# Eight token-major projections of a two-part transformer kernel, taken two weight units at a time with 512 moving columns

## The chip, the cores and the metric

The kernel runs as one program on one core of a Trainium2 chip. The metric is the device time of one execution in microseconds (us), and lower is better. The page and the trace describe one profiled execution; the time before is a median over three executions that were not profiled.

## What is computed

The input is one sequence of 256 tokens with 1024 features and a memory of the same size. A first block of two layers (modulated feed-forward, a mixer of three kinds, feed-forward) is followed by a second block of four layers. Only the second block is touched by the change. Each of its layers is a mixer, a cross attention and a feed-forward, all in fp32:

```python
def second_block(x, mem, ...):
    mem_n = rmsnorm(mem, norm_mem)
    for i in range(DEPTH_2):                        # 4 layers
        hn = rmsnorm(x, norm_mix[i])
        if kind == 0:   mix = diff_attention(hn, da_w_in[j], da_w_out[j], ...)   # q, k, v = split(h @ w_in)
        elif kind == 1: mix = hgrn2(hn, hg_w_in[j], hg_w_out[j], ...)            # q, f, i, g = split(h @ w_in)
        else:           mix = chunked_sgu(hn, sg_w_in[j], sg_w_out[j], ...)      # u, v = split(gelu(h @ w_in))
        x = x + mix
        x = x + mem_cross_attention(rmsnorm(x, norm_cross[i]), mem_n, ca_w_q[i], ca_w_kv[i], ca_w_o[i])
        x = x + swiglu(rmsnorm(x, norm_ffn[i]), ffn_w_gu[i], ffn_w_down[i])
```

Layers 0 and 3 have the differential attention, layer 1 the gated recurrence (hgrn2), layer 2 the gating unit (sgu).

## The kernel before, in words

**Weights in units.** All weight matrices pass through a ring of four slots (`raw`, `whi`, `wlo`; `SLOTS = 4`). A unit is 256 columns of a matrix with 1024 rows: 128 partitions times 2048 elements, 1 MB. For each unit SP (the sync engine) starts a DMA into `raw`. ACT (ScalarE) rounds it to fp32r into `whi` (line 667) and DVE (VectorE) writes the rest, raw minus the rounded value, into `wlo` (line 971). Activations are kept in the same two parts (`hhi`, `hlo`; for the memory `mhi`, `mlo`). A product is then three fp32r matmuls: high by high, high by low, low by high.

**When a unit is split.** ACT and DVE each walk through the same list of stages in program order. At each unit `u` they call `ahead(u.pos)`, which splits units up to three positions ahead. The unit at position `p + 3` lies in the slot that unit `p - 1` used. Both engines therefore wait for `used` of unit `p - 1`, the semaphore that PE (TensorE) raises with that unit's last matmul. DVE waits for ACT's `whi` too. After this call the engine waits for `used` of unit `p` and copies its PSUM bank out (`take_out`). On each engine these things happen strictly one after the other.

**Projections.** `project` runs the units of one projection on PE; `unit` does one of them. Most are feature-major: the weights are stationary and the 256 tokens move (lines 1511 to 1513). Eight are token-major: a 128-token slice of the activations is stationary and the 256 weight columns move (lines 1542 to 1544). They are `dv` in layers 0 and 3, `hv` in layer 1, `sv` in layer 2 and `xv`, the values of the cross attention, in all four layers. Each has four units, and each unit has 48 matmuls: two token tiles, eight row tiles, three products. The two token tiles fill the two halves of one PSUM bank, the bank of the unit's slot. DVE copies `dv`, `hv` and `xv` out (line 1181), ACT copies `sv` out through Gelu (line 767). The first block has token-major units too (`c_v`, `mv`), with the same function.

**What follows a token-major projection.** After `dv` PE starts the attention (`diff`, scores at lines 1791 and 1792), after `hv` the recurrence (`tree8`, line 1684). Both first wait for `all_read`, that is, for every bank of the stage to be copied out. After `sv`, stage `sgu`, ACT waits for the same, squares `sv` (line 906) and takes a root of the sum (lines 909 and 911). DVE meanwhile masks a weight (line 1437), PE turns it (line 1502), DVE copies it (line 1440) and then scales `sv` (line 1444). After `xv` the units of `xq` follow, and nothing waits for the copies at once.

Of the kernel before, what the change touches and what calls it, by code (L numbers as in the profile page):

```python
# [25 lines left out]
ACT = mybir.ActivationFunctionType  # L26
AX = mybir.AxisListType

P = 128
D = 1024  # L30
KT = D // P
S = 256
ST = S // P
# [176 lines left out]
def build(nc, a, out):  # L210

    ctx = ExitStack()
    with ctx:
        def sb(name, shape, dt=F32):
            return ctx.enter_context(nc.sbuf_tensor(name, shape, dt))

        def sem(name):
            return ctx.enter_context(nc.semaphore(name))
# [3 lines left out]
        whi = sb("whi", [P, SLOTS, UNIT], F32R)  # L222
        wlo = sb("wlo", [P, SLOTS, UNIT], F32R)
# [21 lines left out]
        ps = ctx.enter_context(nc.psum_tensor("ps", [P, 8, 512], F32))  # L245
# [13 lines left out]
        def work(at, *dims):  # L259
            n = int(np.prod(dims))  # L260
            v = W[:, at:at + n]
            if len(dims) == 2:
                return v.rearrange("p (a b) -> p a b", a=dims[0])
            if len(dims) == 3:
                return v.rearrange("p (a b c) -> p a b c", a=dims[0], b=dims[1])
            return v
# [30 lines left out]
        dq, dk, dv = work(0, KT, S), work(2048, KT, S), work(4096, ST, D)  # L297
# [3 lines left out]
        hq, hk, hf, hv = work(0, KT, S), work(2048, KT, S), work(4096, KT, S), work(6144, ST, D)  # L301
# [3 lines left out]
        su, sv = work(0, KT, S), work(2048, ST, D)  # L305
# [3 lines left out]
        xk, xv, xq = work(2048, KT, S), work(4096, ST, D), work(6144, KT, S)  # L309
# [6 lines left out]
        used = [sem(f"unit_used{i}") for i in range(SLOTS)]  # L316
        read = [sem(f"bank_read{i}") for i in range(SLOTS)]
        q = {n: sem(n) for n in (
            "const_in mem_in token_in rows_in misc_in bias_out aux_in "
            "rows_turned misc_turned bias_mm vec_copied tok_turned tok_copied pro_v pro_s c_ready "  # L320
            "ada_sum ada_red ada_col "
            "norm_sq norm_ss norm_ln norm_rs norm_gain norm_t norm_hi norm_lo "
            "ffn_hi ffn_lo ffn_scale x_new "
            "gn_sq gn_ss gn_ln gn_rs gn_out rope_mm rope_cos rope_done "
            "gate_mm gate_s gate_v taps_v conv_mm conv_v conv_s conv_hi conv_lo "
            "scores_mm masked maxed exped scaled probs turned_mm turned values_mm values_hi values_lo "
# [62 lines left out]
        for l in range(DEPTH1):  # L389
# [3 lines left out]
            w = a["mix_w_in"][l]  # L393
# [13 lines left out]
        for i in range(DEPTH2):  # L407
            norm("norm_mix_2", i, ready, 2)
            j = i // 3
            if i % 3 == 0:  # L410
                w = a["da_w_in_2"][j]
# [6 lines left out]
            elif i % 3 == 1:  # L418
                w = a["hg_w_in_2"][j]
# [9 lines left out]
            else:  # L429
                w = a["sg_w_in_2"][j]  # L430
# [33 lines left out]
        def bank_read(u):  # L464
            return read[u.slot], u.read + 1

        def product_of(u):
            return used[u.slot], u.use + 1

        def split_ahead(split):  # L470


            at = [0]
            last = {}

            def ahead(pos, far=AHEAD):
                while at[0] < n_stream and at[0] <= pos + far:
                    s, use, _, size = plan.stream[at[0]]
                    if last.get(s, -1) >= max(pos, 0):
                        return  # L480
                    split(s, use, size)
                    last[s] = at[0]
                    at[0] += 1
            return ahead
# [32 lines left out]
        def rows2(v):  # L517
            return v.rearrange("p (a b) -> p a b", a=2)
# [125 lines left out]
        @block_.gpsimd  # L644
        def _(pool):
            nc.gpsimd.memset(gate_w[96:128, :, :], 0.0).then_inc(q["pro_s"], 1)
            for s, use, _, size in plan.stream:
                if s in LO_ON_DVE:
                    continue

                pool.wait_ge(hi_done[s], use + 1)
                if use > 0:
                    pool.wait_ge(used[s], use)
                nc.gpsimd.tensor_tensor(wlo[:, s, 0:size], raw[:, s, 0:size], whi[:, s, 0:size].bitcast(F32),
                                        ALU.subtract).then_inc(lo_done[s], 1)
# [3 lines left out]
        def _(act):  # L659
# [63 lines left out]
            def ffn(st):  # L723
# [23 lines left out]
                "hq": (ACT.Silu, 1.0, lambda i: hq[:, 2 * i:2 * i + 2, :]),  # L747
                "hgate": (ACT.Silu, 1.0, lambda i: h_gate[:, 2 * i:2 * i + 2, :]),
                "su": (ACT.Gelu, 1.0, lambda i: su[:, 2 * i:2 * i + 2, :]),
                "sv": (ACT.Gelu, 1.0, lambda i: sv[:, :, 256 * i:256 * i + 256]),  # L750
                "xk": (ACT.Copy, 1.0, lambda i: xk[:, 2 * i:2 * i + 2, :]),
                "xq": (ACT.Copy, 0.0625, lambda i: xq[:, 2 * i:2 * i + 2, :]),
            }
# [206 lines left out]
        def _(dve):  # L960
            v = nc.vector
# [186 lines left out]
            def outp(st):  # L1148
# [13 lines left out]

            COPIES = {
                "c_v": lambda i: c_v, "mv": lambda i: mv[:, :, 256 * i:256 * i + 256],
                "dv": lambda i: dv[:, :, 256 * i:256 * i + 256], "hv": lambda i: hv[:, :, 256 * i:256 * i + 256],
                "xv": lambda i: xv[:, :, 256 * i:256 * i + 256],
            }

            def take_out(u):
                ahead(u.pos)  # L1170
                name, i = u.what
                if name == "hf":

                    dve.wait_ge(*bank_read(u))
                    for k in (2 * i, 2 * i + 1):
                        ts(hf[:, k, :], hf[:, k, :], lower[:, 1, k:k + 1], lower[:, 0, k:k + 1], ALU.mult, ALU.add)
                        m = ts(hk[:, k, :], hk[:, k, :], lower[:, 1, k:k + 1], None, ALU.mult)
                    m.then_inc(q["mix_f"], 1)
                if name in COPIES:
                    dve.wait_ge(*product_of(u))  # L1180
                    v.tensor_copy(COPIES[name](i), rows2(ps[:, u.slot, :])).then_inc(read[u.slot], 1)
# [315 lines left out]
        def _(pe):  # L1497
            mm = nc.tensor.matmul
# [5 lines left out]
            def weights(u):  # L1504
                pe.wait_ge(hi_done[u.slot], u.use + 1)
                pe.wait_ge(lo_done[u.slot], u.use + 1)

            def product(dst, w, xh, xl, first, last):

                wh, wl = w  # L1510
                mm(dst, wh, xh, start=first, stop=False)  # L1511
                mm(dst, wh, xl, start=False, stop=False)  # L1512
                return mm(dst, wl, xh, start=False, stop=last)  # L1513

            def tiles(slot, cols=256):

                return [t[:, slot, 0:KT * cols].rearrange("p (k m) -> p k m", k=KT) for t in (whi, wlo)]

            def h_parts(src):
                return (mhi, mlo) if src == "mem" else (hhi, hlo)  # L1520

            def unit(u, src, h, extra=()):
                weights(u)

                if u.read > 0:
                    pe.wait_ge(read[u.slot], u.read)
                for e in extra:
                    pe.wait_ge(*e)
                if src == "mem":
                    pe.wait_ge(q["norm_lo"], 8)  # L1530
                xh, xl = h_parts(src)
                th, tl = tiles(u.slot, u.cols)
                for m in range(u.cols // P if not u.token_major else ST):
                    for k in range(KT):
                        if src == "h" and h is not None and m == 0:

                            pe.wait_ge(q["norm_lo"], 8 * h + k + 1)
                        c = slice(P * m, P * m + P)
                        dst = ps[:, u.slot, 256 * m:256 * m + 256]
                        if u.token_major:  # L1540
                            first, last = k == 0, k == KT - 1
                            mm(dst, xh[:, k, c], th[:, k, :], start=first, stop=False)  # L1542
                            mm(dst, xh[:, k, c], tl[:, k, :], start=False, stop=False)  # L1543
                            o = mm(dst, xl[:, k, c], th[:, k, :], start=False, stop=last)  # L1544
                        else:
                            o = product(dst, (th[:, k, c], tl[:, k, c]), xh[:, k, :], xl[:, k, :], k == 0, k == KT - 1)
                o.then_inc(used[u.slot], 1)

            def ada_pair(u, s=0):

                pe.wait_ge(q["ada_sum"], 8 * (u + 2))
                for c in range(2):
                    for t in range(2):
                        at = 2 * (u + c) + t
                        dst = ps[:, 3, at:at + 1] if isinstance(u, int) else ps[:, 3, bass.ds(at, 1)]
                        o = mm(dst, ada_acc[:, 2 * s + c, P * t:P * t + P], ones[:, 0:1], start=True, stop=True)
                o.then_inc(q["ada_red"], 2)
# [104 lines left out]
                outs(STEPS - 1, last=True)  # L1662

            def project(st):
                for n, u in enumerate(st.units):
                    unit(u, st.src, st.h, st.free if n == 0 else ())

            def group_sum(g, bank, src, what):
                pe.wait_ge(q["gn_sq"], g + 1)
# [243 lines left out]
```

## Time and profile before

| | |
|---|---|
| time, median of 3 runs | 3364.84 us (3359.9 to 3366.36) |
| the profiled execution, own time | 3366.07 us |
| its span, first to last instruction | 3364.3 us |
| outside the span | 1.8 us |
| mean granted TensorE clock | 0.928 of full speed |
| busy PE / DVE / ACT | 87% / 55% / 42% of the span |

In the rows below, PE is TensorE's matmul, PEld its weight load, which runs beside it. A matmul's duration in the trace is longer than its share of the stream, since matmuls overlap; what a matmul costs is the distance from its start to the start of the next one. PEclk is the granted clock as a share of full speed: 1.00 is 2.4 GHz and 0.50 is 1.2 GHz. "L1181" is a line of the kernel.

### The profile page before, as it was taken

Reading aid. Unit: us, or ns where it says so; the run is one execution under the profiler, and the core shown is the slowest. Engines: PE = TensorE matmul, PEld = TensorE weight load, DVE = VectorE, ACT = ScalarE, POOL = GpSimd, SP = SyncE. Lnnn points to the kernel's source line nnn. Section 1 sums busy time; section 2 is a strip of 40 time slices with the busy share of each in tenths; the row PEclk is TensorE's granted clock in tenths of the full one; section 3 lists DMA queues with packets and bytes.
Section 4 is the critical chain, followed back from the end, with each engine's and each line's share of the span. In section 5 each row is a group of like instructions: output and inputs, shape, how many; then the busy total and the mean of one; then the engine's idle time right before and its main releaser. Section 6 shows DMA issues by size and latency. Waiting matters only on the chain.

```text
span 3364.3 us, 53426 instructions
## 1 busy us (share of the span) xinstructions
PE 2940.6 (87%) x22527; PEld 2827.3 (84%) x22527; DVE 1841.3 (55%) x2554; ACT 1403.1 (42%) x1620; POOL 0.7 (0%) x5
## 2 busy tenths in 40 slices
PE   3898878989987799859899877999889898969898
PEld 2898858989985799849899876899889898859898
DVE  5786756868758444544444563444444445444443
ACT  3334534344354433454433414444434444344433
POOL 0000000000000000000000000000000000000000
PEclk6899979999997899969999998999989999979999
DMA  6896306968851265515264513345534356414353
GB/s 182 272 299 217 113 26 230 301 206 286 270 181 33 85 204 175 176 37 162 71 206 162 177 54 110 101 150 187 175 126 138 115 185 198 140 50 138 118 183 100
DMA packets 458657, 533.07 MB, mean 158 GB/s; under 512 B 9863, under 2 KB 434937, under 8 KB 458489
## 3 DMA queue, kind: packets, MB, share of 16 engines
q1 hardware_dynamic: 458489, 530.76, 48.7%
q8 instruction: 114, 1.87, 0.2%
q14 instruction: 54, 0.44, 0.0%
HBM read 528.10 MB, written 2.62 MB: 158 GB/s over the span
## 4 chain that ended last, share of the span: by engine, by line
PE 80%; DVE 10%; ACT 5%; DMA 3%; issue 2%; SPq 1%; DVEq 0%; ACTq 0%
PE ps L1511 17%; PE ps L1512 17%; PE ps L1513 17%; PE ps L1640 15%; PE ps L1602 2%; PE ps L1544 2%; PE ps L1543 2%; PE ps L1542 2%; PE ps L1684 2%; DVE work L1093 1%; DVE wlo L971 1%; DMA bias_rows<-raw 1%; DVE work L1258 1%; DMA work<-in_ada_w 1%; PE ps L1670 1%
## 5 line engine op out<-in xcount | busy, mean ns | idle before, releaser
L1511 PE MATMUL ps<-hhi,whi 128*128 128x256 f32 x4528 | 1309.9, 289 | 134.9 <-DVE hlo L1103 85.6
L971 DVE TENSOR_TENSOR wlo<-raw,whi 128x2048 fp32r<-128x2048 f32 (+1 forms) x514 | 976.3, 1920 | 763.0 <-ACT whi L667 762.8
L1512 PE MATMUL ps<-hlo,whi 128*128 128x256 f32 x4528 | 1301.3, 287 | 0.0
L1513 PE MATMUL ps<-hhi,wlo 128*128 128x256 f32 x4528 | 1300.4, 287 | 0.0
L667 ACT ACTIVATE whi<-raw 128x2048 fp32r<-128x2048 f32 (+1 forms) x514 | 824.9, 1613 | 683.5 <-PE ps L1513 396.8
L1511 PEld LDWEIGHTS ps<-hhi,whi 128*128 128x128 f32 x4528 | 891.1, 197 | 150.7 <-issue 150.0
L1512 PEld LDWEIGHTS ps<-hlo,whi 128*128 128x128 f32 x4528 | 890.9, 197 | 1.0 <-issue 1.0
L1513 PEld LDWEIGHTS ps<-hhi,wlo 128*128 128x128 f32 x4528 | 889.9, 197 | 0.0
L1640 PE MATMUL ps<-ghi,whi 128*128 128x256 f32 x1408 | 400.1, 284 | 12.3 <-DVE glo L1119 9.7
L1640 PE MATMUL ps<-glo,whi 128*128 128x256 f32 x1408 | 399.1, 283 | 0.0
L1640 PE MATMUL ps<-ghi,wlo 128*128 128x256 f32 x1408 | 399.0, 283 | 0.0
L1640 PEld LDWEIGHTS ps<-ghi,whi 128*128 128x128 f32 x1408 | 270.9, 192 | 13.7 <-DVE glo L1119 11.0
L1640 PEld LDWEIGHTS ps<-glo,whi 128*128 128x128 f32 x1408 | 271.0, 192 | 0.0
L1640 PEld LDWEIGHTS ps<-ghi,wlo 128*128 128x128 f32 x1408 | 271.0, 192 | 0.0
L730 ACT ACTIVATE work<-ps 128x512 f32<-128x512 f32 x88 | 52.6, 598 | 383.3 <-PE ps L1513 383.3
L1056 DVE SCALAR_TENSOR_TENSOR work<-work,silu_c 128x256 f32<-128x256 f32 x504 | 202.6, 478 | 0.0
L767 ACT ACTIVATE work<-ps 128x512 f32<-128x512 f32 (+1 forms) x74 | 43.8, 592 | 323.4 <-PE ps L1513 310.0
L1602 PE MATMUL ps<-work,con 128*128 128x256 f32 x320 | 101.8, 488 | 57.8 <-ACT work L703 57.8
L1602 PEld LDWEIGHTS ps<-work,con 128*128 128x128 f32 x320 | 79.0, 253 | 77.3 <-ACT work L703 40.5
L738 ACT ACTIVATE ghi<-work 128x512 fp32r<-128x512 f32 x88 | 55.8, 634 | 178.0 <-PE ps L1640 145.2
L1116 DVE TENSOR_TENSOR work<-work,ps 128x512 f32<-128x512 f32 x88 | 60.4, 686 | 123.8 <-PE ps L1513 110.2
L1119 DVE TENSOR_TENSOR glo<-work,ghi 128x512 fp32r<-128x512 f32 x88 | 60.8, 691 | 80.9 <-ACT ghi L738 80.9
(225 smaller groups left out, 2921.3 us busy)
## 6 DMA issues: line engine op xcount, KB each, us to landing
raw<-in_ffn_w_in SPq DMA_DIRECT2D x88, 1024.0 KB, 8.8
raw<-in_ffn_w_gu SPq DMA_DIRECT2D x88, 1024.0 KB, 5.0
work<-in_ada_w SPq DMA_DIRECT2D x72, 1024.0 KB, 8.7
raw<-in_ffn_w_out SPq DMA_DIRECT2D x88, 512.0 KB, 5.6
raw<-in_ffn_w_down SPq DMA_DIRECT2D x88, 512.0 KB, 5.4
raw<-in_ca_w_kv SPq DMA_DIRECT2D x32, 1024.0 KB, 5.4
raw<-in_mix_w_in SPq DMA_DIRECT2D x24, 1024.0 KB, 5.5
raw<-in_da_w_in SPq DMA_DIRECT2D x24, 1024.0 KB, 5.2
```

The source lines that it names most:

```text
L667: f(whi[:, s, 0:size], raw[:, s, 0:size], ACT.Copy).then_inc(hi_done[s], 1)
L971: tt(wlo[:, s, 0:size], raw[:, s, 0:size], whi[:, s, 0:size].bitcast(F32), ALU.subtract).then_inc(lo_done[s], 1)
L1056: m = stt(acc, w, silu_c[:, k:k + 1], acc, ALU.mult, ALU.add)
L1511: mm(dst, wh, xh, start=first, stop=False)
L1512: mm(dst, wh, xl, start=False, stop=False)
L1513: return mm(dst, wl, xh, start=False, stop=last)
L1542: mm(dst, xh[:, k, c], th[:, k, :], start=first, stop=False)
L1543: mm(dst, xh[:, k, c], tl[:, k, :], start=False, stop=False)
L1544: o = mm(dst, xl[:, k, c], th[:, k, :], start=False, stop=last)
L1602: o = mm(ps[:, st.bank, 0:S], ones, norm_x[:, k, :], start=k == 0, stop=k == KT - 1)
L1640: o = mm(dst, a_, b_[:, t, :], start=first and t == 0 and i == 0 and m % 2 == 0, stop=last and t == 1 and i == 2 and m % 2 == 1, skip_grou ...
L1684: o = mm(d[:, c], K[rows_, tile, c], Q[rows_, tile, c], start=True, stop=True)
```

## The change

Within the eight token-major projections of the second block, two neighbouring units are now done together. A new function `unit_pair` waits for the weights and the banks of both units. It then takes the token tiles as the outer loop, and each matmul moves 512 columns: 256 of one slot and 256 of the next. Token tile 0 goes to the bank of the first slot, tile 1 to the bank of the second. Only the very last product of a pair is done as two matmuls of 256 columns, and these raise `used` for the two units. `take_out` copies one bank per token tile, with as many elements as before. The units of the first block keep the old function.

```diff
-                "sv": (ACT.Gelu, 1.0, lambda i: sv[:, :, 256 * i:256 * i + 256]),
+                "sv": (ACT.Gelu, 1.0, lambda i: sv[:, i % 2, 512 * (i // 2):512 * (i // 2) + 512]),
...
-                "dv": lambda i: dv[:, :, 256 * i:256 * i + 256], "hv": lambda i: hv[:, :, 256 * i:256 * i + 256],
-                "xv": lambda i: xv[:, :, 256 * i:256 * i + 256],
             }
+            PAIRED = {"dv": dv, "hv": hv, "xv": xv}
...
+                if name in PAIRED:
+                    t, c = i % 2, 512 * (i // 2)
+                    dve.wait_ge(*product_of(u))
+                    v.tensor_copy(PAIRED[name][:, t, c:c + 512], ps[:, u.slot, :]).then_inc(read[u.slot], 1)
...
+            def unit_pair(u, v, src, h, extra=()):
+                weights(u)
+                weights(v)
+                for w in (u, v):
+                    if w.read > 0:
+                        pe.wait_ge(read[w.slot], w.read)
...
+                xh, xl = h_parts(src)
+                s = u.slot
+                th, tl = (w[:, s:s + 2, :].rearrange("p s (k m) -> p s k m", k=KT) for w in (whi, wlo))
+                for t in range(ST):
+                    c = slice(P * t, P * t + P)
+                    for k in range(KT):
+                        if src == "h" and h is not None and t == 0:
+                            pe.wait_ge(q["norm_lo"], 8 * h + k + 1)
+                        mm(ps[:, s + t, :], xh[:, k, c], th[:, :, k, :], start=k == 0, stop=False)
+                        mm(ps[:, s + t, :], xh[:, k, c], tl[:, :, k, :], start=False, stop=False)
+                        if t == 0 or k < KT - 1:
+                            mm(ps[:, s + t, :], xl[:, k, c], th[:, :, k, :], start=False, stop=k == KT - 1)
+                            continue
+                        for n, w in enumerate((u, v)):
+                            mm(ps[:, s + t, 256 * n:256 * n + 256], xl[:, k, c], th[:, n, k, :], start=False,
+                               stop=n == 1).then_inc(used[w.slot], 1)
...
             def project(st):
-                for n, u in enumerate(st.units):
-                    unit(u, st.src, st.h, st.free if n == 0 else ())
+                us = st.units
+                for n, u in enumerate(us):
+                    extra = st.free if n == 0 else ()
+                    if not u.token_major:
+                        unit(u, st.src, st.h, extra)
+                    elif u.what[1] % 2 == 0:
+                        unit_pair(u, us[n + 1], st.src, st.h, extra)
```

On PE, in the first `dv` projection, this is the place where the third unit begins; `unit_hi`, `unit_lo` and `bank_read` are the semaphores for a split slot and a copied bank. Before:

```order
L1544 MATMUL ps<-whi,hlo 128x256
L1542 MATMUL ps<-whi,hhi 128x256 [waits bank_read2,norm_lo,unit_lo2,unit_hi2]
L1543 MATMUL ps<-wlo,hhi 128x256
L1544 MATMUL ps<-whi,hlo 128x256
L1542 MATMUL ps<-whi,hhi 128x256 [waits norm_lo]
```

And now, where the second pair begins:

```order
L1576 MATMUL ps<-whi,hlo 128x256 x2
L1570 MATMUL ps<-whi,hhi 128x512 [waits bank_read2,unit_lo3,bank_read3,unit_hi3,norm_lo,unit_lo2,unit_hi2]
L1571 MATMUL ps<-wlo,hhi 128x512
L1573 MATMUL ps<-whi,hlo 128x512
L1570 MATMUL ps<-whi,hhi 128x512 [waits norm_lo]
```

The first matmul now waits for both slots and both banks, and no unit boundary follows until the end of the projection.

On DVE, this is the end of the same projection and the start of `diff`; `unit_used` is PE's `used`. Before:

```order
L1181 COPY work<-ps 128x2x256 [waits unit_used0]
L971 TENSOR_TENSOR wlo<-raw,whi 128x2048 [waits unit_used0,unit_hi0]
L1181 COPY work<-ps 128x2x256 [waits unit_used1]
L971 TENSOR_TENSOR wlo<-raw,whi 128x2048 [waits unit_used1,unit_hi1]
L1181 COPY work<-ps 128x2x256 [waits unit_used2]
L971 TENSOR_TENSOR wlo<-raw,whi 128x2048 [waits unit_used2,unit_hi2]
L1181 COPY work<-ps 128x2x256 [waits unit_used3]
```

And now:

```order
L1181 COPY work<-ps 128x512 [waits unit_used0]
L971 TENSOR_TENSOR wlo<-raw,whi 128x2048 [waits unit_used0,unit_hi0]
L1181 COPY work<-ps 128x512 [waits unit_used1]
L971 TENSOR_TENSOR wlo<-raw,whi 128x2048 [waits unit_used1,unit_hi1]
L1181 COPY work<-ps 128x512 [waits unit_used2]
L971 TENSOR_TENSOR wlo<-raw,whi 128x2048 [waits unit_used2,unit_hi2]
L1181 COPY work<-ps 128x512 [waits unit_used3]
```

The order on DVE is the same; what moved is the moment at which `unit_used2` is raised: with the second-last matmul of the projection, where it used to be one unit earlier.

## Rows read from the trace of the kernel before

**Rows 1.** The page: busy times; then the chain that ended last, by engine.

```profile
PE 2940.6 (87%) x22527; PEld 2827.3 (84%) x22527; DVE 1841.3 (55%) x2554; ACT 1403.1 (42%) x1620; POOL 0.7 (0%) x5
...
PE 80%; DVE 10%; ACT 5%; DMA 3%; issue 2%; SPq 1%; DVEq 0%; ACTq 0%
```

**Rows 2.** Windows: two of the eight token-major projections (dv, xv).

```profile
core 0: us, PE busy (x) PEld busy (x) DVE busy (x) ACT busy (x) POOL busy (x), PEclk, DMA share, GB/s
1412.10:1435.20 23.10, 23.10 (x194) 23.01 (x192) 11.24 (x7) 8.15 (x5) 0.00 (x0) 1.00 0.58 184
1560.00:1583.30 23.30, 23.30 (x194) 23.25 (x194) 14.71 (x22) 10.96 (x14) 0.00 (x0) 1.00 0.34 112
```

**Rows 3.** PE in order of time: start us, duration us; first and last of dv.

```profile
1412.12 0.28 PE L1542 MATMUL ps<-whi,hhi 128*128 128x256 f32 x1
...
1435.04 0.28 PE L1544 MATMUL ps<-whi,hlo 128*128 128x256 f32 x1
1436.30 0.50 PE L1791 MATMUL ps<-work 64*128 64x128 f32 x4 [0.99 <-DVE work L1181]
```

**Rows 4.** PE in order of time, fp32r matmuls in a stretch at PEclk 0.50.

```profile
1660.84 0.41 PE L1511 MATMUL ps<-hhi,whi 128*128 128x256 f32 x1
...
1661.27 0.41 PE L1513 MATMUL ps<-hhi,wlo 128*128 128x256 f32 x1
```

**Rows 5.** PE in order of time, plain fp32 matmuls at PEclk 1.00.

```profile
1615.63 1.89 PE L1875 MATMUL ps<-work 128*128 128x256 f32 x8
1617.36 0.60 PE L1502 MATMUL ps<-con,work 128*128 128x128 f32 x4
```

**Rows 6.** The chain at the end of the first dv: start us, duration us, what.

```profile
1435.35 0.70 DVE work L1181
1436.05 0.25 issue
1436.30 0.50 PE ps L1791 x4
1436.80 0.45 PE ps L1792 x4
```

**Rows 7.** DVE, then ACT, in order of time, last unit of that dv.

```profile
1431.61 2.29 DVE L971 TENSOR_TENSOR wlo<-raw,whi 128x2048 fp32r<-128x2048 f32 x1 [1.32 <-ACT whi L667]
...
1429.65 1.92 ACT L667 ACTIVATE whi<-raw 128x2048 fp32r<-128x2048 f32 x1 [3.84 <-PE ps L1544]
```

**Rows 8.** The chain at the end of hv and the start of tree8.

```profile
1940.50 0.70 DVE work L1181
1941.20 0.35 issue
1941.55 3.82 PE ps L1684 x32
```

**Rows 9.** ACT, then DVE, in order of time, end of sv and sgu.

```profile
2465.18 1.90 ACT L667 ACTIVATE whi<-raw 128x2048 fp32r<-128x2048 f32 x1
2470.43 0.60 ACT L767 ACTIVATE work<-ps 128x512 f32<-128x512 f32 x1 [3.36 <-PE ps L1544]
2471.15 1.06 ACT L906 ACTIVATE work<-work 128x1024 f32<-128x1024 f32 x1
...
2469.32 1.22 DVE L1437 TENSOR_TENSOR work<-work,con 128x1024 f32<-128x1024 f32 x1
2471.29 1.29 DVE L1440 COPY work<-ps 128x512 f32<-128x512 f32 x2 [0.75 <-PE ps L1502]
2476.63 1.42 DVE L1444 TENSOR_SCALAR work<-work,stat 128x1024 f32<-128x1024 f32 x2 [4.06 <-ACT stat L911]
```

**Rows 10.** PE around an idle stretch of 6 us; and scores of diff at PEclk 0.50.

```profile
1659.43 0.55 PE L1511 MATMUL ps<-hhi,whi 128*128 128x256 f32 x1 [6.01 <-DVE hlo L1103]
...
1464.46 0.74 PE ps L1791 x4
1465.20 0.85 PE ps L1792 x4
```

More of the change, by code:

```diff
@@ L1547, in unit @@
                 o.then_inc(used[u.slot], 1)
+            def unit_pair(u, v, src, h, extra=()):
[4 more added lines that the diff above has]
+                        pe.wait_ge(read[w.slot], w.read)
+                for e in extra:
+                    pe.wait_ge(*e)
+                if src == "mem":
+                    pe.wait_ge(q["norm_lo"], 8)
+                xh, xl = h_parts(src)
[14 more added lines that the diff above has]
+                               stop=n == 1).then_inc(used[w.slot], 1)
             def ada_pair(u, s=0):
```

## The prediction

> **What bounds the kernel now.** I read the page first: PE is busy for 87% of the span and holds 80% of the chain that ended last [rows 1]. So an instruction of PE inside a long stretch of matmuls costs what it takes, and the gaps between the stretches cost as much. Next I looked at the eight projections that the change touches, in windows. PE is busy without a break in them, PEclk is 1.00, and DVE and ACT are busy for 8 to 15 of some 23 us [rows 2]. The other six windows look the same. So PE bounds these projections, at full clock throughout. DMA is busy at 0.34 to 0.58 in them and has room.
>
> Third, the spacing. The first `dv` matmul starts at 1412.12 and the last, the 192nd, at 1435.04 [rows 3]. That is 22.92 us for 191 steps, or 0.120 us for 256 columns. At 2.4 GHz 256 columns need 256 / 2.4 = 0.1067 us, so 0.013 us per matmul is something else. At half clock the same kind of matmul is spaced 0.43 / 2 = 0.215 us [rows 4], just what 256 columns need at 1.2 GHz (0.213). So at half clock the stream of columns sets the pace, and at full clock a second limit of 0.120 us lies just above it.
>
> **What the wide matmul costs.** A projection has 4 x 48 = 192 matmuls before. Afterwards it has two pairs of 47 wide ones and 2 of 256 columns. The trace has no fp32r matmul of 512 columns. The nearest row is plain fp32: the program's four matmuls of 256 columns stand there as eight records, and they take (1617.36 - 1615.63) / 8 = 0.216 us each [rows 5]. At 2.4 GHz 0.213 us is 512 columns, so TensorE can pass that much per weight load with 0.003 us lost. The bounds are these. From below, 0.216. From above, 2 x 0.120 = 0.240, if fp32r columns themselves only pass at 256 per 0.120 us. Between them, 0.120 + 0.107 = 0.227, if a weight load slows only the part of the stream that runs beside it. I take 0.216. An fp32r stream that was slow by itself should not keep the exact column rate at half clock unless its limit is a rate in absolute time, and then the plain fp32 records would be expected to lose more than 0.003 us. A cost per weight load fits both.
>
> With 0.216 a projection takes 94 x 0.216 + 4 x 0.120 = 20.78 us instead of 192 x 0.120 = 23.04. That is 2.26 us less, and 8 x 2.26 = **18.1 us gained**. With 0.227 it is 21.82 and the gain 9.8 us. With 0.240 it is zero.
>
> The Trainium skill, "TensorE: Matmul & The Clock Gate", section "Back-to-back issue gap", gives N / 2.4 + 2.5 ns at full clock. That is 109 ns for 256 columns and 216 ns for 512, and by it widening would bring only 94 x 2 ns per projection, 1.5 us in all. The trace agrees with the page for the fp32 records (0.216) and disagrees for fp32r at 256 columns (0.120, not 0.109). The same skill, "SBUF — State Buffer", section "Who interferes with whom", gives the moving operand and the weight load read ports of their own, which would speak against a loss from reading side by side. No run here shows that.
>
> **What the change moves: the end of each projection.** Before, `used` of the third unit came 5.76 us (48 x 0.120) before the end. ACT split the slot from 1429.65, 1.92 us, and DVE from 1431.61, 2.29 us [rows 7]. DVE was done at 1433.90, still 1.1 us before PE's last matmul started, so this cost nothing. Only one copy was left: it ran 1435.35 to 1436.05, and PE went on at 1436.30, 1.26 us after its last start [rows 3, 6].
>
> Now `used` of the third unit comes with the second-last matmul, and DVE keeps its order: copy, split, copy. Counted from the start of the last matmul: ACT starts rounding at +0.25. DVE makes its first copy meanwhile (0.70). DVE can start the split 1.96 us after ACT's start (1431.61 - 1429.65), at +2.2, and ends it at +4.5. Then come the second copy, 0.70, and PE's start 0.25 later: +5.4. So PE is idle some 5 us, and the price is 5.4 - 1.26 = 4.15 us. Behind this wait stand both PE's scores and, on DVE and ACT, everything in `diff`, for these need the scores. It applies to `dv` twice and to `hv` once, where `tree8` waits in the same way (copy at 1940.50, PE at 1941.55) [rows 8]: 3 x 4.15 = **12.5 us lost**.
>
> In `sgu` ACT does the copies. Before, the last Gelu copy started at 2470.43 and the squares at 2471.15 [rows 9]. Taking the last matmul's start 0.31 before that copy, as in `dv` (1435.35 - 1435.04) [rows 3, 6], that is 2470.12, from which I count. Now the order is first copy, rounding of 1.90 us, second copy, so the squares begin at 0.19 + 0.50 + 1.90 + 0.72 = +3.3 instead of +1.03: **2.3 us lost**. DVE's side comes out level. Its split ends at +4.9, the mask (1.22) at +6.1, and the turn and copies, 2.0 us before (from about 0.7 before 2471.29 to 2472.58), at +8.1 to +9. It meets the root, which moves from +6.5 to +8.8 (line 1444 was at 2476.63).
>
> After `xv` nothing is lost. PE goes on with the `xq` units, whose slots are split after the end of a pair: about 7.5 us are needed for both slots by the same steps (to +4.5, a copy of 0.70, a split of 2.29), and a pair lasts 10.4 us. The same holds between the first pair and the second in every projection. The start of a pair asks for the second unit's weights 5.76 us earlier than before; these were split two units earlier, so that is free. The number of copies, splits and DMAs is unchanged, and so is their length.
>
> **The clock.** After an idle stretch of 6.01 us PE's first matmuls ran at 0.50 [rows 4, 10]. The new idle stretches are 5 us, where the old ones were about 1 us. So I expect the scores or the first level to run at half clock more often. The first scores take 0.50 + 0.45 = 0.95 us at full clock [rows 6] and 0.74 + 0.85 = 1.59 at half clock [rows 10]: 0.64 us for each of two. The first level of `tree8`, 3.82 us [rows 8], would take about 3 us more. That is 0 to 4.3 us together; I take **4 us lost**, since 5 us is nearer to 6.01 than to 1.
>
> **Sum.** -18.1 + 12.5 + 2.3 + 4 = +0.7 us. The profiled execution took 3366.07 us, its span of 3364.3 and 1.8 around it, so it would take 3366.8. It lies 1.23 us above the median; against the median the forecast is 3365.5 us. What this kernel's measurement can tell from no change is about 0.2%, 6.7 us, so this is no change: the gain in the stream is handed back at the ends. Clock steps falling elsewhere may move it by some 4 us either way.
>
> **Rivals.**
>
> 1. *The fp32r stream is the limit, 0.240 us per 512 columns.* For it: 0.120 is exactly repeated over 191 steps. Against it: rows 4 and 5. The gain is nil and the ends still cost 12.5 + 2.3 + 4: 3364.84 + 18.8 = 3383.6 us, **slower**. The turning point is about 0.225: there the gain is 94 x 8 x 0.015 = 11 us and the result leaves the band of 0.2%.
>
> 2. *Half of the loss stays, 0.227.* Gain 9.8: +9.0 us, 3373.8 us, just slower. Only the skill's port rule speaks against it directly.
>
> 3. *The ends cost nothing.* If ACT and DVE got to the last splits before the second copy is asked for, or PE did not wait for the last bank, the 14.8 us and the clock's 4 would fall away and 3364.84 - 18.1 = 3346.7 us remain, **faster**. Against it: the order on DVE is fixed, and rows 6 show PE released by exactly this copy. It would need the wait on `used` to be shorter than the order of semaphores says.
>
> 4. *The page's spacing.* If 0.109 held for 256 columns, nearly no gain could come (1.5 us) and the time would be about that of the first rival. The measured 0.120 excludes it as a reason; I give it no chance of its own.
>
> **How the numbers follow.** The forecast (0.216, ends paid) has 0.53, of which 0.45 falls within 0.2% and 0.04 on each side through the clock. Rival 1 has 0.25 (slower). Rival 2 has 0.10, of which 0.08 slower and 0.02 within. Rival 3 has 0.12, of which 0.11 faster and 0.01 within. Sums: faster 0.15, same 0.48, slower 0.37. The range reaches down to 3357, the lower end of the forecast with a kind clock, and up to 3385 to take in rivals 1 and 2. It leaves out rival 3 and little else. The forecast's own range is 3359 to 3371.
>
> **What would show it.** Spacing of the wide matmuls: 0.216 (right), 0.227 or 0.240 (rivals 2, 1). A projection's matmuls from first to last start: 20.7 us. PE's gap between the last token-major matmul and the first score or level: 5.4 us, released by DVE's second copy, with a split of 2.29 us between the two copies. Squares in `sgu` 3.3 us after the last matmul. PEclk of 0.50 in the first level of `tree8`. The prediction is wrong if that gap stays near 1.3 us, or if a gap appears between the two pairs or before `xq`, where I expect none.

## The result, and the profile of the changed kernel

The changed kernel takes 3373.24 us, the median of 20 runs (3367.89 to 3377.7). The kernel before takes 3362.59 us in its 20 runs (3359.74 to 3369.01). The ratio is 1.0028, with a 95% interval of 1.0022 to 1.0034. That is **10.7 us slower**, a little beyond the 0.2% that was called no change. The forecast of 3365.5 us was 7.7 us too low. The time lies inside the range of 3357 to 3385, above the forecast's own range of 3359 to 3371, and within 0.6 us of the 3373.8 us of rival 2. The forecasts started from a median of 3364.84 us, 2.3 us above that of the 20 runs, so the changes compare less kindly: +0.7 us forecast, +9.0 by rival 2, +10.7 measured.

The profiled execution has a span of 3372.0 us, against 3364.3 before. The page's busy line, which answers to [rows 1]:

```profile
PE 2935.1 (87%) x21775; PEld 2791.0 (83%) x21775; DVE 1840.0 (55%) x2554; ACT 1400.7 (42%) x1620; POOL 0.7 (0%) x5
```

PE has 752 matmuls fewer (8 projections, 94 fewer in each) and is busy for only 5.5 us less, while the span is 7.7 us longer. So PE is idle for 13.2 us more.

Two windows: first the same `dv` projection as in [rows 2], then the end of `hv` with the start of `tree8`. Columns are the window, its length, busy time and count of PE, PEld, DVE, ACT and POOL, then PEclk, DMA share and GB/s.

```profile
1412.20:1434.20 22.00, 22.00 (x100) 18.09 (x98) 8.16 (x6) 6.15 (x5) 0.00 (x0) 1.00 0.53 174
1940.90:1952.30 11.40, 6.22 (x33) 6.05 (x33) 3.58 (x3) 4.99 (x3) 0.00 (x0) 0.70 0.39 128
```

In the projection PE is still busy without a break at full clock, and PEld no longer is: 18.09 of 22.00 us. In the second window PE is busy for 6.22 of 11.40 us, at a mean clock of 0.70: the clock fell to 0.50 at 1944.69, while PE was idle, and came back at 1951.52.

**The wide matmuls.** PE in order of time, in the second pair of `dv` (start us, duration us, engine, line, what):

```profile
1425.19 0.39 PE L1570 MATMUL ps<-whi,hhi 128*128 128x512 f32 x1
1425.41 0.39 PE L1571 MATMUL ps<-wlo,hhi 128*128 128x512 f32 x1
1425.64 0.39 PE L1573 MATMUL ps<-whi,hlo 128*128 128x512 f32 x1
1425.87 0.39 PE L1570 MATMUL ps<-whi,hhi 128*128 128x512 f32 x1
```

Three matmuls start in 0.68 us, so one costs **0.227 us**, and this is the median of all wide ones in the program. 512 columns need 0.2133 us at 2.4 GHz; the rest is 0.0133 us, the same amount as at 256 columns (0.120 - 0.1067). From first to last start a projection now takes 21.71 us in `dv`, `hv` and `sv` and 21.90 in `xv`, against 22.92 and 23.10. That is 1.2 us less in each, **9.7 us** in eight.

**The end of `dv`.** PE, then ACT, then DVE, in order of time; these rows answer to [rows 3, 6, 7]:

```profile
1433.80 0.40 PE L1576 MATMUL ps<-whi,hlo 128*128 128x256 f32 x2
1439.27 0.62 PE L1826 MATMUL ps<-work 64*128 64x128 f32 x4 [5.07 <-DVE work L1181]
...
1434.18 1.91 ACT L667 ACTIVATE whi<-raw 128x2048 fp32r<-128x2048 f32 x1 [7.19 <-PE ps L1576]
...
1434.12 0.69 DVE L1181 COPY work<-ps 128x512 f32<-128x512 f32 x1 [3.81 <-PE ps L1576]
1436.12 2.29 DVE L971 TENSOR_TENSOR wlo<-raw,whi 128x2048 fp32r<-128x2048 f32 x1 [1.31 <-ACT whi L667]
1438.33 0.68 DVE L1181 COPY work<-ps 128x512 f32<-128x512 f32 x1
```

The last matmul, the second of the two narrow ones, starts at 1433.92 (1433.80 + 0.12). DVE copies the first bank. Then it waits for ACT's rounding, splits a slot for 2.29 us, and only then copies the second bank, for which PE has been waiting. PE goes on 5.35 us after its last start, where it was 1.26 us before.

PE then works on the first scores (lines 1826 and 1827, the L1791 and L1792 of before) at a lower clock: 0.57 on average from 1439.27 to 1441.00. After the first three groups of scores PE turns what DVE has made of them (L1505, the L1502 of before). PE, first before, then now, behind the first and the second `dv`:

```profile
1436.30 0.50 PE L1791 MATMUL ps<-work 64*128 64x128 f32 x4 [0.99 <-DVE work L1181]
1443.05 0.90 PE L1502 MATMUL ps<-con,work 128*128 128x128 f32 x3 [3.71 <-DVE work L1397]
```

```profile
1446.56 0.90 PE L1505 MATMUL ps<-con,work 128*128 128x128 f32 x3 [3.24 <-DVE work L1400]
...
2937.54 0.81 PE L1826 MATMUL ps<-work 64*128 64x128 f32 x4 [5.07 <-DVE work L1181]
2945.02 0.90 PE L1505 MATMUL ps<-con,work 128*128 128x128 f32 x3 [3.25 <-DVE work L1400]
```

From the first score to this turn it takes 6.75 us before and 7.29 and 7.48 us now: **1.3 us more** in the two stages.

**The end of `hv`.** PE, answering to [rows 8]:

```profile
1940.73 0.40 PE L1576 MATMUL ps<-whi,hlo 128*128 128x256 f32 x2
1946.30 6.29 PE L1719 MATMUL ps<-work 128*128 128x128 f32 x32 [5.18 <-DVE work L1181]
```

The gap is 5.46 us (before 1.37), and the 32 matmuls of the first level then take 6.29 us, where they took 3.82: **2.5 us more**. The granted clock is 0.59 on average over these 6.29 us; it was 1.00 before.

**The end of `sv`.** ACT, then DVE, answering to [rows 9]:

```profile
2474.61 0.60 ACT L767 ACTIVATE work<-ps 128x512 f32<-128x512 f32 x1 [6.22 <-PE ps L1576]
2475.11 1.90 ACT L667 ACTIVATE whi<-raw 128x2048 fp32r<-128x2048 f32 x1
2476.91 0.59 ACT L767 ACTIVATE work<-ps 128x512 f32<-128x512 f32 x1
2477.61 1.06 ACT L906 ACTIVATE work<-work 128x1024 f32<-128x1024 f32 x1
...
2483.14 1.41 DVE L1447 TENSOR_SCALAR work<-work,stat 128x1024 f32<-128x1024 f32 x2
```

Here the copies through Gelu stand on either side of the rounding. The last matmul started at 2474.41. The squares begin at +3.2 us, and the scaling (L1447, the L1444 of before) at +8.7. From that last start to the first matmul of the next stage it takes 24.48 us, against 22.29 before: **2.2 us more**.

**After `xv`.** PE, the end of the first `xv` and the start of `xq`:

```profile
1585.34 0.40 PE L1576 MATMUL ps<-whi,mlo 128*128 128x256 f32 x2
1585.57 0.28 PE L1514 MATMUL ps<-hhi,whi 128*128 128x256 f32 x1
```

The last matmul of `xv` starts at 1585.45, the first of `xq` 0.12 us later. No gap appears there or between the pairs.

The parts are -9.7 in the projections, 3 x 4.09 = +12.3 at the ends of `dv` (twice) and `hv`, +1.3 in the scores, +2.5 in the first level of `tree8` and +2.2 in `sgu`, together +8.6 us. The two profiled spans differ by 7.7 us. The medians differ by 10.7: the profiled execution of before (3366.07 us) lies 3.5 us above the median of its 20 runs, that of after 0.5 us above. So some 2 us of the measured change are in none of the parts.

### The profile page after: what moved, and what is told of

Same layout as the page of the kernel before. It is cut to its first block and busy times, and to the rows that moved or that the text cites. A ratio compares the mean times of both kernels' runs of the same rounds, so it can differ in the third digit from the quotient of the medians.

```text
span 3372.0 us, 51906 instructions
## 1 busy us (share of the span) xinstructions
PE 2935.1 (87%) x21775; PEld 2791.0 (83%) x21775; DVE 1840.0 (55%) x2554; ACT 1400.7 (42%) x1620; POOL 0.7 (0%) x5
## 5 line engine op out<-in xcount | busy, mean ns | idle before, releaser
L1670 PE MATMUL ps<-ghi,whi 128*128 128x256 f32 x1408 | 400.0, 284 | 14.5 <-DVE glo L1119 9.7
L1670 PEld LDWEIGHTS ps<-ghi,whi 128*128 128x128 f32 x1408 | 270.9, 192 | 15.9 <-DVE glo L1119 11.0
```

What stands on the lines that cost most here:

```text
L1670: o = mm(dst, a_, b_[:, t, :], start=first and t == 0 and i == 0 and m % 2 == 0, stop=last and t == 1 and i == 2 and m % 2 == 1, skip_grou ...
```

## The experiments

All comparisons are with the kernel before, run on the same chip. Spacing means the distance from one matmul's start to the next one's. The letters of the theories are those used in the expectations.

### Pairs without the wide matmul

```diff
-    mm(ps[:, s + t, :], xh[:, k, c], th[:, :, k, :], ...)      # and the other two products, 512 columns
+    for n, w in enumerate((u, v)):
+        dst = ps[:, s + t, 256 * n:256 * n + 256]
+        mm(dst, xh[:, k, c], th[:, n, k, :], ...)              # and the other two products, 256 columns
```

> The changed kernel with its pairs, waits and copies, but every matmul of a pair moves 256 columns instead of 512 (192 per projection, as before the change). It undoes the widening alone. Theory A (widening gives 0.0133 us per wide matmul, 10 us in all; the ends of dv, hv and sv cost 14.8 us, the clock up to 4): spacing 0.120 us, PE idle about 5 us after dv and hv, time 3362.6 + 14.8 + 0 to 4 = 3377 to 3381 us, ratio to the kernel before 1.0045 to 1.0055. Theory B (the widening gives nothing, the ends cost only about 10 us): the time of the changed kernel, 3373 us, ratio 1.003.

Measured: 3380.43 us against 3364.54, ratio 1.0055 (1.0039 to 1.0070). PE at the end of `dv`:

```profile
1431.16 0.28 PE L1574 MATMUL ps<-whi,hlo 128*128 128x256 f32 x1
1436.27 0.81 PE L1825 MATMUL ps<-work 64*128 64x128 f32 x4 [4.83 <-DVE work L1181]
```

The spacing is 0.120 us again, and the gap is 5.11 us. So the pairing by itself costs 15.9 us. From the parts: 3 x 3.85 at the ends of `dv` and `hv` (gaps of 5.11 and 5.22), 1.4 in the scores (7.47 us to the turn in both stages, against 6.75), 1.4 in the first level of `tree8` (4.95 us from first to last start, against 3.53) and 1.9 in `sgu`, together 16.3. The difference to the changed kernel, 1.0055 - 1.0028 = 0.0027 or 9 us, is what the wide matmuls bring. Its interval is some 5 us on either side, and the 9.7 us read from the rows lie inside it.

### Pairs with the last split moved behind the copies

```diff
 def take_out(u):                     # on DVE; on ACT the same for "sv" alone
-    ahead(u.pos)
     name, i = u.what
+    if name not in ("dv", "hv", "sv", "xv") or i != 3:
+        ahead(u.pos)
```

> The changed kernel, wide matmuls kept, but at the last unit of each token-major projection the look-ahead split is left out (on DVE for all, on ACT for sv), so that the two copies follow each other and the split is done by the next stage. Theory A (the loss sits in the split between the two copies): PE goes on 0.2 + 0.6 + 0.7 + 0.25 = 1.8 us after its last matmul of dv and hv instead of 5.4, the squares of sgu start at about +1.5 instead of +3.3, and the time is 3362.6 - 10 + 3 x 0.5 + 0.5 = 3354 to 3356 us, ratio 0.9975 to 0.998. Theory B (the loss is elsewhere: clock, other stages): gap shorter but time still about 3370 us.

Measured: 3355.6 us against 3364.54, ratio **0.9969** (0.9957 to 0.9981). PE, then DVE, at the end of `dv`:

```profile
1433.28 0.40 PE L1578 MATMUL ps<-whi,hlo 128*128 128x256 f32 x2
1435.14 0.50 PE L1828 MATMUL ps<-work 64*128 64x128 f32 x4 [1.46 <-DVE work L1183]
...
1433.60 1.29 DVE L1183 COPY work<-ps 128x512 f32<-128x512 f32 x2 [3.81 <-PE ps L1578]
```

Both copies now run one after the other, and PE's gap is 1.75 us. In `hv` it is 1.85 us, and the first level of `tree8` is back at 3.81 us. The first scores are back at 6.74 us to the turn, and in `sgu` the squares begin at +1.4 us. So the order on DVE and ACT was the loss at the ends, all but the 0.5 us of the second copy, and with it the loss of clock in the scores and that level. Both kernels are beaten: 9 us faster than before.

Whole stages say the same. From the last start of `dv`, `hv`, `sv` and `dv` to the next feature-major projection it takes 18.5 us more in the changed kernel than before (four stages together), 14.5 with pairs of narrow matmuls, and 0.1 with the split moved. With the 9.7 us saved in the projections that is -9.6 us here, for the 8.9 measured.

### Pairs, and the first bank copied while the second fills

The last split stays moved here, as in the kernel above.

```diff
+    o = mm(ps[:, s + t, :], xl[:, k, c], th[:, :, k, :], ...)
+    if t == 0 and k == KT - 1:
+        o.then_inc(q["tile_done"], 1)
...
-    dve.wait_ge(*product_of(u))
+    dve.wait_ge(*(product_of(u) if t else (q["tile_done"], tile_no(u))))     # ACT: the same for "sv"
```

> late_split, and in addition PE tells of each pair's first token tile with a semaphore of its own when that tile is complete, half a pair before the end, so that the first bank is copied beside the second tile's matmuls. At the end one copy is left, as in the kernel before. Theory A: PE goes on 1.26 us after its last matmul of dv and hv, as before the change; no loss is left, 3362.6 - 10 = 3352 to 3354 us, ratio 0.997 to 0.9975. If late_split's remaining loss was something else than the second copy, it is no faster than late_split.

Measured: 3352.8 us against 3363.43, ratio 0.9969 (0.9957 to 0.9981). DVE, then PE, at the end of `dv`:

```profile
1428.92 0.69 DVE L1192 COPY work<-ps 128x512 f32<-128x512 f32 x1
1432.94 0.69 DVE L1192 COPY work<-ps 128x512 f32<-128x512 f32 x1 [3.33 <-PE ps L1589]
...
1432.50 0.40 PE L1589 MATMUL ps<-whi,hlo 128*128 128x256 f32 x2
1433.89 0.50 PE L1839 MATMUL ps<-work 64*128 64x128 f32 x4 [0.99 <-DVE work L1192]
```

The gap is 1.27 us, as before the change, and the four stages together take 0.6 us less than before. The trace shows the 0.5 us gained at each of three ends, but the two intervals are the same, so the timing can't tell this kernel from the one without `tile_done`.

### Only `xv` in pairs

```diff
+    elif u.what[0] != "xv":
+        unit(u, st.src, st.h, extra)
     elif u.what[1] % 2 == 0:
         unit_pair(u, us[n + 1], st.src, st.h, extra)
```

> Only the four xv projections are taken in pairs with 512 columns; dv, hv and sv are as before the change. After xv nothing waits for the copies. Theory A: no new idle time anywhere, 4 x 1.25 us gained, 3362.6 - 5 = 3357.6 us, ratio 0.9985. Theory B (pairs cost something in the cross attention too): ratio 1.000 or above.

Measured: 3360.04 us against 3364.54, ratio 0.9990 (0.9981 to 0.9999). No gap appears before `xq` or between the pairs. Four projections at 1.2 us are 4.8 us, and 4.5 were measured. So where nothing waits for the copies at once, a pair costs nothing at its end.

### The wide operand in one piece

```diff
+    at = min(256 * k, 1536)
+    wh, wl = whi[:, s, at:at + 512], wlo[:, s, at:at + 512]    # one slot, 512 neighbouring columns
-    mm(ps[:, s + t, :], xh[:, k, c], th[:, :, k, :], ...)
+    mm(ps[:, s + t, :], xh[:, k, c], wh, ...)
```

> The changed kernel, but the wide matmuls read their 512 moving columns from one slot in one piece, instead of 256 from each of two slots. The output is therefore wrong: these projections use other weights. It asks only for the spacing. Theory A (a fixed 0.0133 us per matmul on top of the columns): 0.227 us as in the changed kernel. Theory C (the second piece of the read costs it, and one piece would be as quick as plain fp32): 0.216 us.

Measured: 3371.96 us (one run). PE in order of time, in `xv`:

```profile
1569.95 0.39 PE L1572 MATMUL ps<-whi,mhi 128*128 128x512 f32 x1
...
1570.63 0.39 PE L1572 MATMUL ps<-whi,mhi 128*128 128x512 f32 x1
```

Again three matmuls in 0.68 us. That the operand comes from two slots costs nothing.

### Fewer stationary or fewer moving columns

The next six kernels change one size in `xv` alone. The first two start from the kernel before.

```diff
+    c = slice(P * m + 64 * h, P * m + 64 * h + 64)             # 64 stationary columns, 256 moving
+    mm(ps[0:64, u.slot, 256 * m:256 * m + 256], xh[:, k, c], th[:, k, :], ...)
```

> The kernel before, with the xv projections alone altered: each matmul has 64 stationary columns instead of 128 and there are twice as many; half of the tokens' values are not computed (the halves go to the same place). The moving side stays 256 columns. Theory D (the 0.0133 us come from the weight load that runs beside the stream): with half a load the spacing falls to 0.109 to 0.114 us. Theory E (a cost of each fp32r matmul whatever its load): 0.120 us stays. Time is about 4 x 22 us longer, since the number of matmuls doubles there.

```diff
+    d = slice(128 * h, 128 * h + 128)                          # 128 stationary columns, 128 moving
+    mm(ps[:, u.slot, 256 * m + 128 * h:256 * m + 128 * h + 128], xh[:, k, c], th[:, k, d], ...)
```

> The kernel before, with the xv projections alone altered: each matmul moves 128 columns instead of 256, twice as many matmuls, same result. It shows what the weight load alone allows. If an fp32r load of 128 columns needs 0.120 us, the spacing stays 0.120 (then the load bounds the kernel before, but the 0.227 of the wide matmul would need another reason). If a load needs 0.107 to 0.112 as for plain fp32, the spacing is that, and 0.120 at 256 columns is the stream of 0.107 plus 0.0133. If the loads were no limit: 0.053 + 0.0133 = 0.067.

Measured: 3446.0 and 3445.83 us, with twice as many matmuls in each `xv`. A stretch of each in order of time, first with 64 stationary columns, then with 128 moving ones:

```profile
1579.74 0.28 PE L1555 MATMUL ps<-whi,mhi 128*64 128x256 f32 x1
...
1580.08 0.28 PE L1555 MATMUL ps<-whi,mhi 128*64 128x256 f32 x1
```

```profile
1579.95 0.27 PE L1556 MATMUL ps<-whi,mhi 128*128 128x128 f32 x1
...
1580.62 0.28 PE L1556 MATMUL ps<-whi,mhi 128*128 128x128 f32 x1
```

With 64 stationary columns three matmuls take 0.34 us. Between neighbours the spacing is 0.1134 us on average, not 0.120. With 128 moving columns six take 0.67 us, 0.112 for one, though the columns alone need 0.0533. So with a weight load of 128 columns the spacing has a floor of about 0.11 us (the same 128 moving columns take 0.060 with a load of 32, below), and a narrower load removes half of the excess at 256 moving columns. The Trainium skill, "TensorE: Matmul & The Clock Gate", section "LDWEIGHTS (loading the stationary operand)", gives P / 1.2 ns for the load, which is 107 ns for 128 columns. The trace's 112 ns are 5 ns above it.

The same in the changed kernel, with 64 stationary and 512 moving columns:

```diff
-    c = slice(P * t, P * t + P)
+    c = slice(P * t, P * t + n_st)                             # n_st = 64 in xv
```

> The changed kernel, but the xv pairs have only 64 stationary columns per matmul (512 moving columns as before, same number of matmuls); half of the tokens' values are left out. Measured so far at 2.4 GHz: 0.120 us for 128 stationary and 256 moving columns, 0.227 for 128 and 512, 0.1135 for 64 and 256. Theory D (the load adds 0.0133 us per 128 stationary columns, whatever is moved): 0.2133 + 0.0067 = 0.220 us. Theory F (the cost of a wide matmul has another cause than the narrow one's): 0.227 us.

Measured: 3377.48 us (one run). PE in order of time:

```profile
1575.02 0.39 PE L1574 MATMUL ps<-whi,mlo 128*64 128x512 f32 x1
1575.25 0.39 PE L1571 MATMUL ps<-whi,mhi 128*64 128x512 f32 x1
1575.47 0.39 PE L1572 MATMUL ps<-wlo,mhi 128*64 128x512 f32 x1
```

The spacing is uneven, 0.224 to 0.237 us, 0.230 on average. That is not the 0.220 that a cost in proportion to the load would give; it is 0.003 more than with the full load. One kernel more on the stationary side:

```diff
+    c = slice(P * m, P * m + 32)                               # 32 stationary columns, 256 moving
+    mm(ps[0:32, u.slot, 256 * m:256 * m + 256], xh[:, k, c], th[:, k, :], ...)
```

> The kernel before, but the xv matmuls have 32 stationary columns and 256 moving ones, same number of matmuls; three quarters of the tokens' values are left out. Theory D: 0.1067 + 0.0033 = 0.110 us. If half of the cost were fixed: 0.113 us as with 64.

Measured: 3355.19 us (one run).

```profile
1570.10 0.28 PE L1554 MATMUL ps<-whi,mhi 128*32 128x256 f32 x1
...
1570.44 0.28 PE L1554 MATMUL ps<-whi,mhi 128*32 128x256 f32 x1
```

Three matmuls in 0.34 us, 0.1133 for one: no less than with 64 columns. So the excess does not go with the size of the load. Two readings were left. Either the columns of these matmuls pass at 256 per 0.1133 us (theory R; then 512 take 0.2267), or each matmul has a fixed cost beside its columns (theory F). Two further sizes tell them apart:

```diff
+    mm(dst, xh[:, k, c], th[:, k, d], ...)                     # kernel before: 32 stationary, 128 moving
```

> The kernel before; in xv alone each matmul has 32 stationary columns and 128 moving ones, 384 matmuls per projection (three quarters of the rows of xv are left out, so its output differs there). With 32 stationary and 256 moving columns the spacing was 0.1133, with 128 stationary and 128 moving 0.1115. Theory R (the columns of these fp32r matmuls pass at 256 per 0.1133 us at 2.4 GHz): 0.0567 per matmul. Theory F (the columns pass at 2.4 GHz, 0.0533 for 128, and each matmul adds a fixed 0.0067 or more): 0.060 to 0.067. If the weight load has a floor of its own that does not shrink with its columns: near 0.11 as before.

```diff
+    d, ah, al = ps[:, s + t, 0:2 * cols], th[:, :, k, 0:cols], tl[:, :, k, 0:cols]    # cols = 192 in xv
+    mm(d, xh[:, k, c], ah, ...)                                # kernel after: 128 stationary, 384 moving
```

> The kernel after; in xv alone the wide matmuls move 384 columns (192 of each slot; a quarter of the columns of xv is left out). 128 stationary columns. Theory F (fixed 0.0133 per matmul beside the columns at 2.4 GHz): 0.160 + 0.0133 = 0.1733. Theory R (256 columns per 0.1133, and nothing more once the load is hidden): 0.170. Something that comes in steps with the number of columns would show as neither.

Measured: 3360.59 and 3350.33 us (one run each, before 3360.62). PE with 32 stationary and 128 moving columns, then with 384 moving ones:

```profile
1577.81 0.22 PE L1556 MATMUL ps<-whi,mhi 128*32 128x128 f32 x1
...
1577.99 0.22 PE L1556 MATMUL ps<-whi,mhi 128*32 128x128 f32 x1
```

```profile
1574.90 0.33 PE L1572 MATMUL ps<-whi,mhi 128*128 128x384 f32 x1
...
1575.42 0.33 PE L1572 MATMUL ps<-whi,mhi 128*128 128x384 f32 x1
```

In both, the two rows are three matmuls apart. The first has a spacing of 0.060 us (theory R: 0.0567), the second 0.1733 us (theory R: 0.170). Both are what theory F gives, with a fixed cost of 0.0067 for a narrow load and 0.0133 for a full one. Theory R falls. All sizes side by side, in a steady stretch at full clock:

| stationary | moving | spacing, us | columns at 2.4 GHz | excess |
|---|---|---|---|---|
| 128 | 128 | 0.112 | 0.0533 | load is the floor |
| 128 | 256 | 0.120 | 0.1067 | 0.0133 |
| 128 | 384 | 0.1733 | 0.1600 | 0.0133 |
| 128 | 512 | 0.227 | 0.2133 | 0.0133 |
| 64 | 256 | 0.1134 | 0.1067 | 0.007 |
| 64 | 512 | 0.230, uneven | 0.2133 | 0.017 |
| 32 | 256 | 0.1133 | 0.1067 | 0.0067 |
| 32 | 128 | 0.060 | 0.0533 | 0.007 |

With 128 stationary columns, as in the eight projections, the excess is a fixed 0.0133 us per matmul from 256 to 512 moving columns. What stays open is the row with 64 stationary and 512 moving columns: its excess is even a little above that of a full load, and no run says why. What the fixed cost consists of is open too.

## Why the prediction was right and where it was wrong

- **What bounds the kernel: right.** PE stayed busy without a break at full clock in the projections, so its spacing counted there, and the gaps between stretches added to the time.
- **The wide matmul: the step that failed, by its size.** The prediction set it to 0.216 us, as plain fp32 matmuls take per record [rows 5], and argued that "a cost per weight load fits both". The measured 0.227 is such a cost per matmul. It was the row taken for its size that misled: the fp32 records lose 0.003 us each, an fp32r matmul with a full load loses 0.0133, whatever its width from 256 columns up. The prediction had the right number in hand. The 0.120 of [rows 3] minus the 0.1067 us of 256 columns is this cost, and 0.2133 + 0.0133 = 0.2267. It was named as the middle bound and got a chance of 0.10 as rival 2, though the row of the same operation should have gone before the row of another data type. The gain was 9.7 us instead of 18.1. These 8.4 us are most of the 10.0 between the forecast change and the measured one. What rival 2 gave as the reason, a load that slows the stream beside it, is not shown: half a load did not lower the 0.227.
- **Rival 1 (0.240): wrong.** From 256 to 384 to 512 columns the spacing grows by 0.0533 us each time, which is 128 columns at 2.4 GHz. So the stream of columns has the full rate.
- **The ends of `dv` and `hv`: right.** A gap of 5.4 us was worked out, and 5.35 and 5.46 came, released by DVE's second copy behind a split of 2.29 us. The loss was 12.3 us for 12.5. Moving the split away took it back, which shows the cause.
- **`sgu`: right.** The squares came at +3.2 (worked out: +3.3), the scaling at +8.7 (+8.8), and 2.2 us were lost for 2.3. With the last split moved the squares came at +1.4.
- **After `xv` nothing: right.** Shown by the kernel with only `xv` in pairs.
- **The clock: right at the ends.** 3.8 us were lost there for the 4 expected. The first level of `tree8` lost 2.5 us, close to the 3 expected. It took 3.53 us from first to last start behind every short gap, and 4.95 to 6.04 behind the long ones. The first scores lost 0.54 us in the first `dv` and 0.73 in the second, for 0.64 expected in each. In all thirteen kernels the way from the first score to the turn takes 6.74 or 6.75 us behind a short gap and 7.29 to 7.48 behind a long one. Over the whole program the time at half clock does not follow the ends: 486 us before, 501 after, 486 with pairs of narrow matmuls and 501 with the last split moved. That part is left out of the account, and some of the 2 us that are in none of the parts may lie there; no run shows it.
- **Rival 3 (the ends cost nothing): not here**, but it is what the moved split brings. It promised 18.1 us less than before; with the measured price of a wide matmul it would be 9.7 us less, and 8.9 and 10.6 were measured.

The sum with the measured price is -9.7 + 12.5 + 2.3 + 4 = +9.1 us, for the 10.7 measured; counted from 3364.84 us it leads to 3373.9. So one term decided most of the miss and the side on which the result fell. That this, like the 3373.8 of rival 2, comes so close to the measured time is luck in part: the median of three runs from which both start lies 2.3 us above that of the 20.

The Trainium skill, "TensorE: Matmul & The Clock Gate", section "Back-to-back issue gap", gives N / 2.4 + 2.5 ns for a single matmul, 216 ns for 512 columns. No fp32r matmul of this kernel reaches it. The same section gives some 81 ns for 128 columns and 131 ns for 512 in a sustained stream; here the traces have 112 and 227 with 128 stationary columns (and 60 for 128 moving columns with 32 stationary), so neither figure holds for fp32r.

## What to carry to other kernels

Price an operation at a new size from the rows of the same operation and data type: subtract the columns' time and keep the rest as a fixed cost, before turning to a row of another kind. When units are merged, look at what the last buffer's release triggers. Two buffers that were freed one after the other are now freed together, and whatever an in-order engine does between the two copies stands in the path of the stage that waits for the last one. Putting both copies before that work turned this change from 0.3% slower into 0.3% faster.

## What the runs showed of the hardware

- An fp32r matmul with 128 stationary columns costs its moving columns at the granted clock plus 0.0133 us, from 256 to 512 columns at full clock. At half clock nothing is left of it: the 0.215 us of [rows 4] are read from two steps, and over 449 steps of the kernel before the median is 0.213, just the 0.2133 that 256 columns need.
- The excess is halved, to 0.007 us, with 64 or with 32 stationary columns at 256 moving ones, but not with 64 at 512.
- With a load of 128 columns the spacing of matmuls with 128 moving columns is 0.112 us. With 32 stationary columns a matmul of 128 moving columns takes 0.060.
- A moving operand in two pieces from two buffers costs the same as one in a single piece (0.227 both).
- After 5.2 us without work (a start-to-start gap of 5.46) PE ran the 32 matmuls of the first level of `tree8` in 6.29 us instead of 3.82; after 1 to 1.6 us idle they kept their 3.8. The gap just before isn't all that counts: in the kernel with the early copy the second level took 5.18 us after an idle stretch of 2.57, with the last split moved 3.81 after 2.58. PE, second level, first of the early copy, then of the moved split:

```profile
1941.90 5.18 PE L1732 MATMUL ps<-work 128*128 128x128 f32 x32 [2.57 <-DVE work L1219]
```

```profile
1945.38 3.81 PE L1721 MATMUL ps<-work 128*128 128x128 f32 x32 [2.58 <-DVE work L1210]
```
